# Moving the softmax normalisation of the last attention to GpSimd, with scores, exponentials and weights one unit further ahead

## The reference

```python
def nsa_layer(x, mem, ...):
    ...
    o_slc = selected_attention(q, ks, vs, p_cmp, slopes)
    o_win, _ = banded_attention(q, kw, vw, slopes, WIN_SIZE - 1, 1)
    gates = jax.nn.sigmoid(gate_logits.astype(jnp.float32)).reshape(b, s, g, r, 3).transpose(0, 2, 3, 1, 4)
    o = gates[..., 0:1] * o_cmp + gates[..., 1:2] * o_slc + gates[..., 2:3] * o_win
    o = o.transpose(0, 3, 1, 2, 4).reshape(b, s, NSA_WIDTH).astype(x.dtype)
    ym = memory_attention(qm, rms_norm_2(mem, mem_norm_g), w_mem_kv)
    y = jnp.concatenate([o * jax.nn.silu(z), ym * jax.nn.silu(zm)], axis=-1)
    return x + (y.astype(x.dtype) @ w_out)
```

## Time and profile before

| | us |
|---|---|
| median of 3 runs | 2018.76 |
| lowest, highest | 2018.72, 2019.66 |
| the profiled execution's own time | 2013.86 |
| its span | 2012.0 |
| start of T(0), start of T(19) (L3223) | 1909.88, 1965.39 |
| first product of `out_stage` (L872) | 1968.65 |

### The profile page before, as it was taken

One profiled execution on the slowest core, in us unless ns is written; L12 is line 12 of the kernel. 1 busy time (PEld: TensorE's weight loads), 2 busy tenths in 40 slices (PEclk: granted clock), 3 DMA queues, 4 the chain that ended last, 5 costly groups with the idle time before them and its releaser, 6 DMA issues.

```text
span 2012.0 us, 26580 instructions
## 1 busy us (share of the span) xinstructions
PE 1691.6 (84%) x11294; PEld 1049.1 (52%) x11294; DVE 606.6 (30%) x1546; ACT 361.9 (18%) x817; POOL 74.2 (4%) x80
## 2 busy tenths in 40 slices
PE   6997879976777667999987776787799998999988
PEld 4756754533333333755544333353378874568753
DVE  1657633211111112662320111111141053311292
ACT  1113213100000001322311100010121223211271
POOL 0000100000000001000000000000100000000000
PEclk9997998988788889999888888898899999999899
DMA  9995326999999999773699999999983343066100
GB/s 352 377 310 209 85 85 255 419 428 428 428 428 429 428 428 409 268 269 123 265 426 422 427 430 428 424 427 428 421 291 139 130 168 115 1 189 201 53 1 32
DMA packets 142766, 582.33 MB, mean 289 GB/s; under 512 B 30940, under 2 KB 42332, under 8 KB 117984
## 3 DMA queue, kind: packets, MB, share of 16 engines
q1 hardware_dynamic: 113504, 558.49, 69.3%
q10 hardware_dynamic: 24000, 10.32, 2.0%
q0 software_dynamic: 5184, 12.43, 1.8%
HBM read 571.41 MB, written 13.11 MB: 291 GB/s over the span
## 4 chain that ended last, share of the span: by engine, by line
PE 50%; DMA 35%; DVE 8%; issue 2%; ACT 2%; PEld 1%; PEldq 1%; SPq 0%; DVEq 0%; ACTq 0%; POOL 0%; POOLq 0%
DMA ring<-in_exp_w_dram 31%; PE bank L735 15%; PE bank L724 6%; PE bank L872 6%; PE bank L2133 5%; PE bank L2497 3%; PE bank L2194 2%; PE bank L2487 2%; DMA ring<-in_hawk_w_mem_kv_dram 1%; PE bank L2139 1%; DMA ring<-in_ada_w_dram 1%; DMA taken_rows<-expert_out,route_rows 1%; PE bank L1999 1%; DVE pair_probs L3273 1%; DVE pair_probs L3258 1%
## 5 line engine op out<-in xcount | busy, mean ns | idle before, releaser
L2133 PE MATMUL bank<-ring,hidden_room 128*32 128x512 f32 x2032 | 291.5, 697 | 165.8 <-DMA ring<-in_exp_w_dram 163.4
L735 PE MATMUL bank<-hT,ring 128*128 128x256 f32 x1344 | 294.0, 381 | 2.6 <-ACTq L167 2.2
L735 PEld LDWEIGHTS bank<-hT,ring 128*128 128x128 f32 x1344 | 256.6, 191 | 39.1 <-issue 2.8
L2133 PEld LDWEIGHTS bank<-ring,hidden_room 128*32 128x32 f32 x2032 | 66.2, 121 | 318.9 <-DMA ring<-in_exp_w_dram 175.8
L2194 PE MATMUL bank<-ring,hidden_room 128*32 128x256 f32 x1984 | 162.4, 481 | 46.7 <-DMA ring<-in_exp_w_dram 30.9
L2394 DVE COPY hidden_room<-bank 128x512 f32<-128x512 f32 x64 | 44.3, 691 | 513.0 <-PE bank L2133 513.0
L2139 PEld LDWEIGHTS bank<-kc,hidden_room 128*128 128x128 f32 x1024 | 133.9, 204 | 73.0 <-issue 65.5
L2139 PE MATMUL bank<-kc,hidden_room 128*128 128x32 f32 x1024 | 141.3, 284 | 3.0 <-DVE hidden_room L2394 1.6
L2194 PEld LDWEIGHTS bank<-ring,hidden_room 128*32 128x32 f32 x1984 | 75.4, 131 | 100.8 <-issue 68.1
L2301 ACT COPY hidden_room<-bank 128x512 f32<-128x512 f32 x64 | 37.5, 586 | 474.8 <-PE bank L2133 474.8
L724 PE MATMUL bank<-ring,hT 128*128 128x512 f32 (+2 forms) x288 | 114.3, 557 | 0.0
(11 more groups left out here) (588 smaller groups left out, 1845.9 us busy)
## 6 DMA issues: line engine op xcount, KB each, us to landing
ring<-in_exp_w_dram SPq DMA_DIRECT2D x189, 2048.0 KB, 26.6
ring<-in_ada_w_dram SPq DMA_DIRECT2D x24, 2048.0 KB, 16.8
ring<-in_hawk_w_in_dram SPq DMA_DIRECT2D x15, 2048.0 KB, 9.2
ring<-in_even_w_in_dram SPq DMA_DIRECT2D x7, 2048.0 KB
ring<-in_gla_w_in_dram SPq DMA_DIRECT2D x6, 2048.0 KB, 20.2
ring<-in_nsa_w_in_dram SPq DMA_DIRECT2D x5, 2048.0 KB, 8.2
ring<-in_even_w_out_dram SPq DMA_DIRECT2D x2, 2048.0 KB
expert_out<-kc POOLq DMA_DIRECT2D x8, 512.0 KB, 9.2
```

What stands on the lines that cost most here:

```text
L735: last = nc.tensor.matmul(pair[m // 2][0:rows, (m % 2) * T:(m % 2 + 1) * T], w[:, k, m * P:m * P + rows], src[:, k, :], start=(k == 0), st ...
L2133: last = nc.tensor.matmul(dst[quarters[k % NQ], :], own[:, q, k % 2, k // 2, :], w[:, k, :], start=(k < NQ), stop=(k >= KD - NQ))
```

## The change

The multiplication of a unit by its weights moves from DVE to GpSimd, which gets a loop of 20 of them. DVE keeps the reciprocal and the gates (`weigh`), and signals GpSimd with a semaphore. The scores go 4 units ahead instead of 3, the exponentials 3 instead of 2, the weights 2 instead of 1. The tiles `pair_probs` and `pair_stat` keep their four slots.

```diff
-            n, AHEAD = len(units), 3
+            n, AHEAD, DEPTH = len(units), 4, 4
...
                         keep_warm(bank[4], 6)
+                        pe.wait_ge(shifted.sem, shifted.at(2))
+                        scores(3)
                         pe.wait_ge(c_norm.sem, c_norm.at(1))
...
-                        def normalize(u):
-                            m, keys = units[u]["parts"], units[u]["keys"]
+                        def weigh(u):
+                            m = units[u]["parts"]
                             dve.wait_ge(exped.sem, exped.at(u + 1))
...
-                            step(nc.vector.reciprocal(w, sums))
-                            if units[u]["gates"] is not None:
-                                step(nc.vector.tensor_tensor(w, w, units[u]["gates"], ALU.mult))
...
-                            nc.vector.tensor_tensor(d, d, wide.unsqueeze(2).to_broadcast([P, 2 * m, keys]), ALU.mult).then_inc(normal.up(), 1)
...
+                            if units[u]["gates"] is None:
+                                nc.vector.reciprocal(w, sums).then_inc(weighed.up(), 1)
+                            else:
+                                step(nc.vector.reciprocal(w, sums))
+                                nc.vector.tensor_tensor(w, w, units[u]["gates"], ALU.mult).then_inc(weighed.up(), 1)
...
-                        normalize(0)
+                        weigh(0)
                         dve.wait_ge(c_turned.sem, c_turned.at(1))
                         nc.vector.tensor_copy(cT[:, :, :, :].rearrange("p t g q -> p (t g q)"), bank[5][:, :]).then_inc(c_in.up(), 1)
+                        weigh(1)
+                        bias_and_low(3)
                         for u in range(n + 1):
...
-                            if u + 1 < n:
-                                normalize(u + 1)
+                            if u + 2 < n:
+                                weigh(u + 2)
...
                         exps(1)
+                        exps(2)
                         for u in range(n):
...
-                            if u + 2 < n:
-                                exps(u + 2)
+                            if u + 3 < n:
+                                exps(u + 3)
+
+                    @block.gpsimd
+                    def _(pool):
+                        for u in range(n):
+                            m, keys = units[u]["parts"], units[u]["keys"]
+                            d = probs[:, u % DEPTH, :, :] if m == 2 else probs[:, u % DEPTH, 0::2, :]
+                            d = d[:, :, 0:keys]
+                            wide = weight[:, u % DEPTH, :] if m == 2 else weight[:, u % DEPTH, 0::2]
+                            pool.wait_ge(weighed.sem, weighed.at(u + 1))
+                            nc.gpsimd.tensor_tensor(d, d, wide.unsqueeze(2).to_broadcast([P, 2 * m, keys]), ALU.mult).then_inc(normal.up(), 1)
```

More of the change, by code:

```diff
@@ L3171, in pair_attention @@
                 c_scored, c_low, c_exp = signal("index_dots_ready"), signal("route_max_ready"), signal("route_exp_ready")
+                weighed = signal("norm_inverse_ready")
                 c_norm, c_turned, c_in = signal("route_weighed"), signal("tiles_turned"), signal("cmp_hidT_ready")
@@ L3181, in seg @@
                 def seg(u, par, part):
-                    return probs[:, u % 4, 2 * par + part, 0:units[u]["keys"]]
+                    return probs[:, u % DEPTH, 2 * par + part, 0:units[u]["keys"]]
                 with Stage(whole, met) as block:
@@ L3258, in bias_and_low @@
                                 ins = nc.vector.tensor_tensor_reduce(seg(u, par, part), score(u, par)[:, part, :], units[u]["heads"][par]["bias"], 1.0, 3e38,
-                                                                     ALU.add, ALU.min, low[:, u % 4, 2 * par + part:2 * par + part + 1])
+                                                                     ALU.add, ALU.min, low[:, u % DEPTH, 2 * par + part:2 * par + part + 1])
                             ins.then_inc(shifted.up(), 1)
-                        def normalize(u):
-                            m, keys = units[u]["parts"], units[u]["keys"]
+                        def weigh(u):
+                            m = units[u]["parts"]
                             dve.wait_ge(exped.sem, exped.at(u + 1))
-                            sums = total[:, u % 4, :].rearrange("p (h b) -> p h b", h=2)[:, :, 0:m]
-                            w = weight[:, u % 4, :].rearrange("p (h b) -> p h b", h=2)[:, :, 0:m]
-                            step(nc.vector.reciprocal(w, sums))
-                            if units[u]["gates"] is not None:
-                                step(nc.vector.tensor_tensor(w, w, units[u]["gates"], ALU.mult))
-                            d = probs[:, u % 4, :, :] if m == 2 else probs[:, u % 4, 0::2, :]
-                            d = d[:, :, 0:keys]
-                            wide = weight[:, u % 4, :] if m == 2 else weight[:, u % 4, 0::2]
-                            nc.vector.tensor_tensor(d, d, wide.unsqueeze(2).to_broadcast([P, 2 * m, keys]), ALU.mult).then_inc(normal.up(), 1)
+                            sums = total[:, u % DEPTH, :].rearrange("p (h b) -> p h b", h=2)[:, :, 0:m]
+                            w = weight[:, u % DEPTH, :].rearrange("p (h b) -> p h b", h=2)[:, :, 0:m]
+                            if units[u]["gates"] is None:
[3 more added lines that the diff above has]
+                                nc.vector.tensor_tensor(w, w, units[u]["gates"], ALU.mult).then_inc(weighed.up(), 1)
                         nc.vector.memset(zeros[:, :], 0.0).then_inc(vector_steps.up(), 1)
@@ L3322, in exps @@
                                 d, i = seg(u, par, part), 2 * par + part
-                                ins = nc.scalar.activation(d, d, ACT.Exp, bias=low[:, u % 4, i:i + 1], scale=-1.0, accum_out=total[:, u % 4, i:i + 1])
+                                ins = nc.scalar.activation(d, d, ACT.Exp, bias=low[:, u % DEPTH, i:i + 1], scale=-1.0, accum_out=total[:, u % DEPTH, i:i + 1])
                             ins.then_inc(exped.up(), 1)
```

4 lines of the change are left out of this document (2 added, 2 removed).

## The result

The kernel before took 2018.76 us (median of 5 runs, 2016.96 to 2021.46), the changed one 2009.24 us (5 runs, 2006.57 to 2011.04): ratio 0.995, 95% interval 0.9933 to 0.9966, so 10.1 us less (6.9 to 13.5). The forecast was 8.0 less, with a range down to 2009.0, which is 9.8 less. The direction and the mechanism inside the stage held. The gain came out larger than forecast: the median of the changed kernel lies 0.2 us inside the range, the ratio puts it at 2008.7, 0.3 us outside, and the second comparison puts it well inside.

The account below looks back on a forecast made before the run. DVE was taken to set the stage's pace, with PE next. PE's floors -9.0, ACT +0.3 and head +0.6 made -8.1, say -8.0 us: from 2018.76 to 2010.8 us, range 2009.0 to 2017.0.

Parts of the forecast that it names:

- DVE bounds, PE is next: In the stage, DVE sets the pace (busy 21.59 of 22 us with long units); once relieved, PE limits.
- PE's floors, -9.0: PE's iteration times without waits, summed from unit 0's transposes to unit 19's: 46.5 us against 55.5 before.
- the restart: Extra 0.20 us charged in iteration 16, which has no scores: 0.63 us less 0.43 for four passes of 256 columns.
- ACT, +0.3: ACT, nearly full at about 2.1 us per short unit, adds 0.1 us to three intervals of the stage.
- Head, +0.6: Ahead of the loop, unit 3's scores stand behind the warm-up and go on the path, costing 0.6 us.
- The sign "T(0) after 1911": Unit 0's transposes starting after 1911 us in the trace would show the prediction wrong.
- GpSimd's multiplication, 2.45 and 1.38 us, hidden up to 2.9 and 1.7: Price on GpSimd per long and short unit, twice DVE's; up to those thresholds PE's iteration hides it.
- "The gain goes through whole": Behind the stage nothing overlaps, as the next begins when all three engines meet; no term for that part.
- Shared port: Rival: DVE and GpSimd exclude each other when both read a second SBUF operand; +6.6 us, 2025.4 us; chance 0.09.
- POOL starts late: Rival: GpSimd's first multiplication pays a one-time start as long as 6 us; net -3, 2015.8 us; chance 0.06.
- That one part would do: In the loop, weights two units ahead were said to give GpSimd's multiplication a full iteration; no separate size given.

Follow-up runs that it names:

- the second comparison: The changed kernel, unedited, measured again against the kernel before: 2009.13 us (8 runs), ratio 0.9958, interval 0.9944 to 0.9972.
- `scores3_late`: Changed kernel with unit 3's scores moved behind the transposes of the compressed attention's weights: 2006.99 us (one run), head 12.54 us in place of 13.32.
- `pool_only`: GpSimd multiplies as in the changed kernel, but scores, exponentials and weights stay 3, 2 and 1 units ahead: 2025.13 us, ratio 1.0045 to the kernel before.

## Why the prediction was right inside the stage, and which step failed

- **DVE bounds, PE is next.** Right. DVE fell from 21.59 to 16.37 us in 22, PE has no gap, and DVE waits for scores.
- **PE's floors, -9.0.** Forecast 46.5 us from T(0) to T(19), measured 46.18. By single distances: iteration 0 1.46 (1.6), short 2.00 to 2.03 (2.03), 4 to 7 2.46 (2.46), iteration 8 2.89 (2.89), 9 to 11 3.33 (3.33), 12 to 15 2.90 (2.90), 16 1.83 (2.04), 17 and 18 1.26 and 1.24 (1.25). Iteration 16 was put too high: the restart was charged with 0.20 us that isn't there.
- **ACT, +0.3.** Wrong: nothing was lost to it, no distance is above its floor. ACT waited for PE (9.5 us), with exponentials now three ahead. Together with the term above, -9.33 in place of -8.7.
- **Head, +0.6.** Measured +0.79, shown to be S(3) by `scores3_late` (-0.78). The first T still waits 0.88 us for the copy of the compressed weights, as in the earlier trace rows. The prediction weighed 0.43 us at full clock against 0.86 at the half level. The clock was up again by then, and S(3) took 0.63: the 0.43 and the restart of 0.20 that the prediction charged in iteration 16 and left out here. The other 0.16 lie at its edges. The 0.6 was a guess between two clock levels, and what it missed was the restart. The sign "T(0) after 1911" did come (1916.90), but only because the stage began later; from S(0), 1911 stands for 13.65 us, and T(0) came at 13.32.
- **GpSimd's multiplication, 2.45 and 1.38 us, hidden up to 2.9 and 1.7.** Measured 1.89 and 1.04; the row of the same instruction on DVE, doubled, was too high, but nothing hung on it. The threshold was borne out as far as tested: 2.93 us of POOL work with a long unit left 3.33, and 3.8 us made POOL the pace. Where between these it lies was not tried. The estimate from the Trainium skill (GPSIMD Engine Reference) was 2.3 and 1.2 us, above the measured ones too.
- **"The gain goes through whole", nothing for what lies behind T(19).** This is the step that failed. Two things differed there, and the sum had neither. The clock fell in three profiled executions of five of the kernel before and in neither of the changed one's two: 1.3 us less on the mean. That the new stage prevents the fall is possible and not shown. And the output's write landed later: 0.95 us more. Together that is 1.8 us less in the profiled pair and 45.2 - 44.8 = 0.4 on the mean.
- **Sum.** -9.33 + 0.79 - 0.4 = -8.9 us, -10.3 with the profiled pair's tail, against a forecast of -8.0. So the terms inside the stage were short by 0.4 us (-8.5 for -8.1) and the part behind T(19) by 0.4 to 1.8. The two comparisons say -10.1 (6.9 to 13.5) and -8.5 (5.6 to 11.3), and both hold the sum. The 1.2 us from -8.9 to -10.1 have no row; they are within the first comparison's interval. On which side of the range's end the first comparison fell was chance: the second, of the same two kernels, fell inside. The low end of the range, 2009.0, lay only 1.8 us under the forecast, while the first comparison's interval alone reaches over 3 us to each side. It was made from terms and had no room for the spread of the runs.
- **Shared port.** It fell for the reason the prediction gave. The bias instructions ran at 0.41 to 0.42 us beside POOL. The exclusion itself is real: two 128x256 products with two SBUF operands beside POOL took back the whole gain (55.59 us), two reductions of the same length with one took nothing.
- **POOL starts late.** It fell: 1.03 us, as later, 0.1 us after DVE's gates. The set-up instruction (MODIFY_POOL_CONFIG, of the same line L3350) ran at 1448.5 us, so if it starts anything, there were 466 us for it. The Trainium skill (GPSIMD Engine Reference, instruction dispatch) has some 6 us for the first call of a freshly loaded routine; no row here shows it.
- **That one part would do.** The prediction treated the depth as what makes room for POOL, and `pool_only` shows that without it the change is slower than before, by 5.9 us in the stage.

## What to carry to other kernels

Moving work off a full engine onto an emptier but slower one lengthens each unit's way, so price the move together with the depth that hides it: here the parts alone were +5.9 and -2.7 us in the stage, and -9.3 together. Then compare what lies behind the stage too, in several executions of each kernel, before it is put at nothing. When the full engine is relieved, read the next engine's floor for each kind of iteration from places where it already ran without a wait; that gave 46.5 for 46.18 us. Before putting work on GpSimd, list which DVE instructions will run beside it with two SBUF operands, and let a forecast's range be at least as wide as the measurement's own spread.

## What the runs showed of the hardware

- A DVE instruction with both operands in SBUF is held while GpSimd's multiplication runs, a tiny one too: 4 elements a partition went from 0.16 to 1.55 us. With one operand in PSUM, or one only, it isn't (0.41 us each). It goes both ways: GpSimd's instruction took 2.01 us in place of 1.89 when it started beside such a product.
- GpSimd's multiplication took 1.89 us for 1024 elements a partition, 1.04 for 512 and 0.61 for 256, about 1.66 ns an element and 0.19 us besides; DVE's 1.23 and 0.69.
- In the same kernel the granted clock fell around the end of the stage in three profiled executions of five, and reached into the last product in two (36.59 and 36.51 us for 34.60), with the stage ahead of it alike to 0.02 us from T(0) to T(19).
- The last write of the program landed after 2.7 us in eleven profiled executions and after 3.6 in seven, the edits being elsewhere. In the seven a packet of the instruction queue ran in the same last 8 us, in the eleven none.
